# Moving the SBUF areas behind the constants by 128 bytes, and widening the constants' array by 96 unused columns

## What is computed

```
z = rmsnorm(x) @ w_in                       # 1024 x 8968
ya, yb, yc, yd = window attention, gated convolution, forgetting attention, block attention of parts of z
x = x + (sum over branches of sigmoid(gates) * (y @ w_br)) @ w_out
x = x + (silu(g) * v) @ w_down              # g, v: short convolution of rmsnorm(x) @ w_up
x = rmsnorm(x)                              # end of the first block
u = rmsnorm(x) @ w_in_2                     # pooling and differential attention on parts of u
x = x + concat(y_pool, y_diff) @ w_out_2
x = x + cross_attention(rmsnorm(x), rmsnorm(mem))
x = x + moe_ffn(rmsnorm(x))                 # 32 experts, 4 of them for each token
y = rmsnorm(x)
```

## Time and profile before

| | |
|---|---|
| median of 3 runs | 1738.22 us |
| the profiled execution, its own time | 1737.07 us |
| its span, first to last instruction | 1735.3 us |
| instructions | 22657 |
| TensorE busy | 1576.9 us (91%) |
| VectorE, ScalarE, GpSimd busy | 753.6, 482.2, 179.0 us |
| moved by DMA | 527.89 MB, mean 304 GB/s |
| mean granted TensorE clock | 0.988 |

### The profile page before, as it was taken

The page is one execution under the profiler, slowest core; times in us unless marked ns, Lnnn a source line. Parts: engine busy times, 40 slices in busy tenths (PEclk is TensorE's granted clock), DMA queues, the critical chain, the costliest instruction groups (busy, mean ns, idle before and its releaser), DMA issues.

```text
span 1735.3 us, 22657 instructions
## 1 busy us (share of the span) xinstructions
PE 1576.9 (91%) x9680; PEld 997.6 (57%) x9680; DVE 753.6 (43%) x1338; ACT 482.2 (28%) x824; POOL 179.0 (10%) x208
## 2 busy tenths in 40 slices
PE   7999999899999998989999888988888888888886
PEld 6998899899999988974333332323232232323222
DVE  6898777779884788552211211111121211111121
ACT  4345566355553553531100100001010100001001
POOL 0301112405530041010000000000000000000000
PEclk9999999999999998998999999999999999999999
DMA  8865455456655644757999999999999999999996
GB/s 222 189 207 143 128 147 170 146 164 182 190 193 173 196 132 151 248 217 268 422 421 421 422 421 422 421 421 421 422 421 421 422 421 422 421 422 422 421 422 277
DMA packets 195001, 527.89 MB, mean 304 GB/s; under 512 B 18545, under 2 KB 136350, under 8 KB 145742
## 3 DMA queue, kind: packets, MB, share of 16 engines
q1 hardware_dynamic: 191008, 519.23, 78.2%
q0 software_dynamic: 3344, 6.93, 2.5%
q10 hardware_dynamic: 542, 0.21, 0.1%
HBM read 524.70 MB, written 1.62 MB: 303 GB/s over the span
## 4 chain that ended last, share of the span: by engine, by line
DMA 44%; PE 41%; DVE 10%; ACT 3%; issue 1%; SPq 0%; DVEq 0%; ACTq 0%
PE bank L604 41%; DMA slot_ring<-in_w_down 15%; DMA slot_late<-in_w_down 8%; DMA slot_high<-in_w_down 8%; DMA slot_memx<-in_w_down 8%; DVE slot_ring_r L1954 2%; DMA slot_ring<-in_w_gu 2%; DMA slot_memt<-in_w_gu 2%; ACT high_r L1525 1%; DMA slot_ring<-in_w_in 1%; DVE stat L2164 1%; DVE conv L1962 0%; DVE slot_late_r L1954 0%; ACT score_fox L1525 0%; ACT score_swa L1525 0%
## 5 line engine op out<-in xcount | busy, mean ns | idle before, releaser
L604 PE MATMUL bank<-h_hi_r,high_r 128*128 128x256 f32 x1000 | 285.7, 286 | 6.9 <-DVE slot_ring_r L1954 5.6
L1954 DVE TENSOR_TENSOR slot_ring_r<-slot_ring,high_r 128x1024 fp32r<-128x1024 f32 x198 | 248.1, 1295 | 81.7 <-ACT high_r L1525 79.1
L604 PE MATMUL bank<-h_lo_r,high_r 128*128 128x256 f32 x1000 | 282.7, 283 | 0.0
L1958 DVE TENSOR_SCALAR ga<-bank 128x512 f32<-128x512 f32 x32 | 22.1, 691 | 588.9 <-PE bank L604 588.9
L604 PE MATMUL bank<-h_hi_r,slot_ring_r 128*128 128x256 f32 x952 | 269.1, 283 | 0.0
L1525 ACT ACTIVATE high_r<-slot_ring 128x1024 fp32r<-128x1024 f32 x198 | 197.9, 1051 | 63.8 <-PE bank L604 42.0
L604 PEld LDWEIGHTS bank<-h_hi_r,high_r 128*128 128x128 f32 x1000 | 191.3, 191 | 9.0 <-DVE slot_ring_r L1954 6.1
L1525 ACT ACTIVATE th_e<-ga 128x512 f32<-128x512 f32 x32 | 20.2, 630 | 621.0 <-DVE ga L1958 621.0
L604 PEld LDWEIGHTS bank<-h_lo_r,high_r 128*128 128x128 f32 x1000 | 191.1, 191 | 0.1
L604 PEld LDWEIGHTS bank<-h_hi_r,slot_ring_r 128*128 128x128 f32 x952 | 182.0, 191 | 0.0
L604 PE MATMUL bank<-slot_ring,xg 128*64 128x512 f32 x528 | 123.9, 601 | 11.9 <-DMA slot_ring<-in_w_gu 11.9
(11 more groups left out here) (438 smaller groups left out, 2900.8 us busy)
## 6 DMA issues: line engine op xcount, KB each, us to landing
slot_ring<-in_w_gu SPq DMA_DIRECT2D x66, 1024.0 KB, 26.9
slot_high<-in_w_gu SPq DMA_DIRECT2D x50, 1024.0 KB, 26.7
slot_ring<-in_w_down SPq DMA_DIRECT2D x49, 1024.0 KB, 26.6
slot_last<-in_w_gu SPq DMA_DIRECT2D x38, 1024.0 KB, 27.1
slot_ring<-in_w_in SPq DMA_DIRECT2D x36, 1024.0 KB, 5.4
slot_late<-in_w_gu SPq DMA_DIRECT2D x32, 1024.0 KB, 26.7
slot_high<-in_w_down SPq DMA_DIRECT2D x25, 1024.0 KB, 27.0
slot_ring<-in_w_up SPq DMA_DIRECT2D x44, 512.0 KB, 4.7
```

The lines of the kernel that those rows point to most:

```text
L604: return e.matmul(o, lhs, rhs, start=start, stop=stop, skip_group_check=True)
L1954: return e.tensor_tensor(o, i, j, op)
L1958: return e.tensor_scalar(o, i, s1, None, op1)
```

## The change

Three edits. The gap between the constants and `COLS` grows from 64 to 96 columns, so everything behind it and up to the areas of the stages lies 128 bytes further in each partition; `AREAS` becomes 32 columns smaller and the upper slots stay. The array `consts` gets columns of zeros until its width is 3 more than a multiple of 128: 1827 columns become 1923, a row is 7692 bytes instead of 7308, the array 984,576 bytes instead of 935,424. The transfer of `diag_const` gets an upper bound, so that it still reads 768 columns.

After the change the starts modulo 256 are 0 for `slot_ring`, `slot_high` (and `high_r`) and everything at `AR` and `QKV`, 160 for `X`, `H`, `HH`, `RSTD` and `slot_h_hi`, and 128 for `POSI`; 128 stays for the constants and the upper slots.

```diff
@@ shape_constants
         parts[name] = e
+
+    parts["unused"] = np.zeros((P, -(sum(a.shape[1] for a in parts.values()) - 3) % P))
     where, at = {}, 0
@@ hybrid_moe_program
         n_const = const_cols["kept"][1]
-        CONST, COLS = 0, -(-n_const // 8) * 8 + 64
+        CONST, COLS = 0, -(-n_const // 8) * 8 + 96
         X = COLS + 4 * P
@@ sync_program
                 if name == ("qa", 0):
-                    e.dma_start(diag_const, a["consts"][:, n_const:]).then_inc(*rest_in.step("rest"))
+                    e.dma_start(diag_const, a["consts"][:, n_const:n_const + 2 * TOEP]).then_inc(*rest_in.step("rest"))
                     e.dma_start(const_sb[:, 2 * P:], a["consts"][:, 2 * P:n_const]).then_inc(*rest_in.step("rest"))
```

## The result

The changed kernel takes 1727.28 us (median of 4 runs, 1723.58 to 1729.69) against 1738.16 us: ratio 0.9931, with a 95% interval of 0.9919 to 0.9943 (the two medians alone give 0.9937). It is 10.9 us faster, 0.6 to 0.7%. The forecast was no change, and the range of 1733 to 1743 us does not hold it. The profiled execution took 1729.69 us and was the slowest of the four; its span is 1727.9 us, 7.4 us less than before.

The account below looks back on a forecast made before the run. Matmuls were taken to bound the first half and DMA engines moving 8 KB pieces the last 840 us. The four parts summed as 0 + 0 + 0 + 0 on 1737.07 us, plus 1.15 us to the median: 1738.2 us, range 1733 to 1743.

Parts of the forecast that it names:

- What bounds the kernel, and the unit: Matmuls first, DMA in the last 840 us; one ns a piece on 157 loads into slot_ring and slot_high is 1.26 us.
- Part 1, the transfers' destinations: Loads into slot_ring, slot_high and slot_h_hi at their new starts modulo 256 bytes: no change in time, 0.
- The near bound: Loads into slot_ring and slot_high: at most 3.3 ns a piece either way, from source-side rows, 4.1 us.
- the far one: Loads into slot_ring and slot_high: an even start saves at most 11.9 ns a piece, 14.9 us.
- The page's rule: Rival on slot writes: bytes ahead of an uneven start are paid for, 4.7 ns a piece, 5.9 us gain; chance 0.04.
- Part 2, the engines: TensorE matmuls and VectorE operations with operands at the new places: no change in time, 0.
- the bound of 0.1 ns: TensorE: at most 0.1 ns on each of some 6000 matmuls ahead of 918 us, 0.6 us.
- Part 3, the constants: Transfers from consts ahead of qa and the stall behind them from 66.89 us: 0, at most 0.2 us either way.
- Part 4, device memory: Weights possibly at new places behind the wider consts array: 0, bounds 3.5 us and 8.9 us on all 336 loads.
- The rival of slower reads: Experts' stream: weights' new device memory places slow all 336 loads, 3.5 us to 8.9 us; chance 0.10.
- The sign given for a gain: Queue of 860 to 1700 us: rate rises 0.5% to 422 or 423 GB/s, slices with more slot_ring and slot_high loads faster.

Follow-up runs that it names:

- e8: Kernel before with all 15 slots, X, H, HH and the small tensors moved to 0 modulo 256 bytes: 1730.31 us, ratio 0.9964.
- e5: Kernel before with a gap of 88 columns for 64, so slot_ring and slot_high start at 224 modulo 256: 1741.07 us, ratio 1.0022.
- e7: Kernel before with 32 unused columns between slot_ring and slot_high, so three of 15 slots at 0 modulo 256: 1732.90 us, ratio 0.9981.

## Why the prediction was wrong, point by point

- **What bounds the kernel, and the unit.** Right. The experts' stream set the end, a ns on each piece into `slot_ring` and `slot_high` was worth 1.26 us, and the 7.7 ns of the table above give 9.7 us by it. The loads one by one have 6 to 7 ns, 8 to 9 us.
- **Part 1, the transfers' destinations.** This is the step that failed: "I take nothing". The term was 157 x 8 x 7.7 ns = 9.7 us. The near bound of 3.3 ns was too small by more than half; the far one of 11.9 ns held. The reasons given for 0 were bad. That a start at 32 and one at 128 cost alike was read as a sign that starts cost nothing, where it only compared two uneven starts; the prediction had said that it tells nothing of 0, and then used it. And the difference on the source's side, which shrinks from 3.3 to 1.3 ns between 512 bytes and 1 KB, was taken to stand for the destination. It does not: on the destination's side an 8 KB piece still pays 6 to 9 ns.
- **The page's rule.** The Trainium skill (DMA: Bandwidth & Descriptors, How a descriptor splits into AXI transactions) pointed the right way, and the rival built on it, 1732.3 us, was the nearest of those that gain by the transfers. Carried over to writes its mechanism is wrong: 224 bytes ahead of the start cost the stream 0.6 us more than 128 did, and not 4.4.
- **Part 2, the engines.** Right for this change: 203.32 us for 203.37, 283 ns and 1220 ns as before. But the bound of 0.1 ns rested on means over the whole span, with falls of the clock in them. In one stretch of the kernel before, 368 to 572 us with the clock at 1.00, the product with `h_lo_r` took 280 ns and that with `ff_lo_r`, an operand in the areas from `AR` on, 283 (both rows above). And e8 shows 3 ns for `h_lo_r` itself in other places, and 2.8 us.
- **Part 3, the constants.** What was called a stall of 15.73 us is the load's time from issue to landing; TensorE lost 0.72 us of idle time to it. Its change was put at 0.2 us either way, and the two profiles of the changed kernel alone differ by 1.06 us in it (17.44 and 16.38). A single profile has this spread, and the prediction did not allow for it.
- **Part 4, device memory.** Right: ratio 1.0011 with the array widened alone, 352.81 MB for 352.79. The rival of slower reads had a chance of 0.10 and widened the range upwards, where nothing was.
- **The sign given for a gain**, 422 or 423 GB/s and slices with more even loads faster than others, was right in kind; the rate was 426.

## What to carry to other kernels

Where transfers of long pieces (8 KB here) into the on-chip memory bound a stage, let their destinations start at a multiple of 256 bytes in the partition; it costs no instruction, and a few unused columns ahead of the buffers do it. Here 7 of 15 even slots brought some nine tenths of what 14 or 15 brought in the stream. When a price is to be bounded by the trace before, ask whether any row holds the new case at all: two rows that agree with each other bound nothing if both lie on the same side of it.

## What the runs showed of the hardware that was not expected

- A load of 8 KB pieces takes 2.485 us with a destination at 32 or 128 modulo 256 bytes, 2.49 at 224, and 2.43 at 0 among uneven loads; with all slots even it takes 2.45. No start between multiples of 32 was tried, and no piece size but 8 KB was timed with even and uneven destinations.
- The same TensorE product takes 280 to 283 ns in kernels that differ only in where their areas lie, with all instructions alike. e5 and e7 show that the distance between moving operand and weights is not what decides.
- A kernel can lose 1 to 3 us in the first 370 us of its span to a load that lands a little later and a fall of the granted clock behind it. The fall of 88 us is in one profile of the changed kernel and not in the other. A difference of 2 to 4 us in the total, as in e5, is to be looked up in the stage that it is claimed for.
